# A two-layer encoder trunk on one Trainium2 core: another order of work at the entry of each feed-forward block, and bank sums ahead of weight splits

## What is computed

```python
def rmsnorm(x, g):
    y = x * lax.rsqrt(jnp.mean(x * x, axis=-1, keepdims=True) + EPS)
    return y * g

def conv_gated_ffn(h, w_up, conv_w, conv_b, w_down):
    a = h @ w_up                                   # (1, 512, 1024) @ (1024, 2 * 2816)
    a = depthwise_conv(a, conv_w, width=3, centred) + conv_b
    gate, val = jnp.split(a, 2, axis=-1)
    return (jax.nn.silu(gate) * val) @ w_down

def trunk(x, ...):
    x = x + dilated_attention_mixer(rmsnorm(x, attn_norm_g), ...)          # layer 0
    x = x + conv_gated_ffn(rmsnorm(x, ffn_norm_g[0]), ...)
    x = x + chunk_gmlp_mixer(rmsnorm(x, gmlp_norm_g), ...)                 # layer 1
    x = x + conv_gated_ffn(rmsnorm(x, ffn_norm_g[1]), ...)
    return x
# reference: trunk(x_prompt), trunk(x_sample), each (1, 512, 1024), fp32, shared weights
```

## Time and profile before

| | us |
|---|---|
| median of 3 runs | 2109.98 (2106.78 to 2114.1) |
| profiled execution | 2112.5 |
| its span, first to last instruction | 2110.3 |

### The profile page before, as it was taken

One profiled execution on the slowest core, in us unless ns is written; L12 is line 12 of the kernel. 1 busy time (PEld: TensorE's weight loads), 2 busy tenths in 40 slices (PEclk: granted clock), 3 DMA queues, 4 the chain that ended last, 5 costly groups with the idle time before them and its releaser, 6 DMA issues.

```text
span 2110.3 us, 24700 instructions
## 1 busy us (share of the span) xinstructions
PE 2046.5 (97%) x9316; PEld 1677.6 (79%) x9316; DVE 1248.0 (59%) x1691; ACT 934.3 (44%) x1441; POOL 324.1 (15%) x234
## 2 busy tenths in 40 slices
PE   8999999998999999999999999999899999999999
PEld 8888677886778778787888888888678778778787
DVE  5398774588666666634535344449766666643333
ACT  6233686645444444423434532344544444432221
POOL 0022000341222222000102000223222222100000
PEclk9999899999999999999999999999999999999999
DMA  5111000412432232344343311142252232244444
GB/s 167 31 40 41 16 16 9 142 50 70 160 90 69 81 90 69 126 144 141 135 157 117 80 41 31 51 140 60 60 170 79 71 90 79 73 147 139 133 148 170
DMA packets 181165, 196.48 MB, mean 93 GB/s; under 512 B 8000, under 2 KB 135488, under 8 KB 181056
## 3 DMA queue, kind: packets, MB, share of 16 engines
q1 hardware_dynamic: 180912, 194.80, 29.2%
q10 hardware_dynamic: 144, 0.21, 0.0%
HBM read 159.33 MB, written 35.65 MB: 92 GB/s over the span
## 4 chain that ended last, share of the span: by engine, by line
PE 79%; DVE 12%; issue 4%; ACT 4%; DMA 1%; POOL 0%; SPq 0%; ACTq 0%; DVEq 0%; POOLq 0%
PE bank L766 16%; PE bank L768 16%; PE bank L767 16%; PE bank L539 6%; PE bank L540 6%; PE bank L541 6%; DVE spl L1411 2%; ACT spl L1154 2%; PE bank L690 2%; DVE gate_out L1674 2%; DVE gate_out L1671 2%; PE bank L718 1%; PE bank L701 1%; DVE bank L1655 1%; PE bank L641 1%
## 5 line engine op out<-in xcount | busy, mean ns | idle before, releaser
L766 PE MATMUL bank<-bh,spl 128*128 128x512 f32 x1064 | 421.9, 397 | 41.2 <-DVE bank L1655 23.8
L767 PE MATMUL bank<-bl,spl 128*128 128x512 f32 x1064 | 417.4, 392 | 0.0
L768 PE MATMUL bank<-bh,spl 128*128 128x512 f32 x1064 | 417.3, 392 | 0.0
L766 PEld LDWEIGHTS bank<-bh,spl 128*128 128x128 f32 x1064 | 201.7, 190 | 98.9 <-DVE bank L1655 39.8
L766 PE MATMUL bank<-hid_h,down_h 128*128 128x512 f32 x704 | 275.4, 391 | 4.5 <-DVE x L1796 4.5
L1411 DVE TENSOR_TENSOR hid_l<-hid_w,hid_h 128x1024 fp32r<-128x1024 f32 x88 | 107.8, 1225 | 287.7 <-ACT hid_h L1294 287.7
L767 PE MATMUL bank<-hid_l,down_h 128*128 128x512 f32 x704 | 275.2, 391 | 0.0
L768 PE MATMUL bank<-hid_h,down_l 128*128 128x512 f32 x704 | 274.9, 391 | 0.0
L768 PEld LDWEIGHTS bank<-bh,spl 128*128 128x128 f32 x1064 | 201.6, 189 | 42.6
L767 PEld LDWEIGHTS bank<-bl,spl 128*128 128x128 f32 x1064 | 201.9, 190 | 41.2
L1294 ACT ACTIVATE hid_h<-hid_w 128x1024 fp32r<-128x1024 f32 x88 | 93.2, 1059 | 311.3 <-DMA down_w<-w_down 311.3
(11 more groups left out here) (210 smaller groups left out, 3798.0 us busy)
## 6 DMA issues: line engine op xcount, KB each, us to landing
raw<-w_up SPq DMA_DIRECT2D x88, 512.0 KB, 5.4
hid_w<-hidden_kept SPq DMA_DIRECT2D x88, 512.0 KB, 3.5
hidden_kept<-hidden SPq DMA_DIRECT2D x88, 256.0 KB, 2.3
down_w<-w_down SPq DMA_DIRECT2D x88, 256.0 KB, 3.8
x_kept<-x SPq DMA_DIRECT2D x16, 512.0 KB, 6.5
x<-x_kept SPq DMA_DIRECT2D x16, 512.0 KB, 8.2
gws<-w_in SPq DMA_DIRECT2D x32, 256.0 KB, 3.2
qws<-w_qkv SPq DMA_DIRECT2D x12, 512.0 KB, 3.9
```

The lines of the kernel that those rows point to most:

```text
L766: mm(out, wh, ah, start=first, stop=False, skip_group_check=True)
L767: mm(out, wh, al, start=False, stop=False, skip_group_check=True)
L768: return mm(out, wl, ah, start=False, stop=last, skip_group_check=True)
```

## The change

It reorders; it adds no arithmetic and removes none. Part by part:

1. **Norm statistics.** `norm_cols` comes one half block (12 matmuls) earlier in TensorE's list and `norm_rows` too. VectorE's 4 normalisations of sequence 1 are moved ahead of `scaled(0, 0)` and read bank 4 in place of `rstd`; job 1 therefore waits before its third block for all 12 normalisations, not 8.
2. **Part sums on GpSimd.** T2 and T4 move from VectorE to GpSimd, whose list is now T1, T2, T3, T4 and then the weight sums of job 3. One semaphore (`b_t`) counts all four. P5 is split before P2's blocks, so the counts in `READY` change.
3. **Bank evictions of jobs 0 to 2** and the weight splits between them have another order on ScalarE and VectorE; block 15's split and P4's ScalarE part stand elsewhere in the list.
4. **Windows, jobs 3 to 21.** On VectorE `c22(j)` stands ahead of `w_lo(n0 + 8)`, and `c12(j)` ahead of `w_lo(n0 + 9)` (in job 21 ahead of the tile splits).
5. **First sweep's eviction.** The 8 `evict` stand behind `tile_lo(23)` and no longer behind `tile_lo(24)`.

```diff
--- before.py
+++ after.py
@@ -88,7 +88,7 @@
 NENT = len(ORDER)
 RING = 4
 
-READY = {P1: 4, P2: 8, P5: 9, P6: 10, P3: 11, P7: 12, P4: 13}
+READY = {P1: 4, P5: 5, P2: 9, P6: 10, P3: 11, P7: 12, P4: 13}
 NB = 13
 NADD = 4 * PLAIN + 3 * NWIN
 
@@ -278,8 +278,7 @@
         b_gain = sem("b_gain")
         b_norm = sem("b_norm")
         b_norm12 = sem("b_norm12")
-        b_t13 = sem("b_t13")
-        b_t24 = sem("b_t24")
+        b_t = sem("b_t")
         b_hi = sem("b_hi")
         b_lo = sem("b_lo")
         cp_t1 = sem("cp_t1")
@@ -795,7 +794,7 @@
                         pe.wait_ge(st_root, layer + 1)
                     if j == 1 and q == 2:
                         pe.wait_ge(st_copy, (layer + 1) * NS)
-                        pe.wait_ge(b_norm, layer * 12 + KD)
+                        pe.wait_ge(b_norm, layer * 12 + 12)
                     if j >= 2 and q == 0:
                         pe.wait_ge(hid, (layer * NUP + j - 1) * 2)
                     if j >= 2 and q == 2:
@@ -809,9 +808,9 @@
                             last = triple(bank[:, ((b, c), (a, d))[q // 2][s]], w[:, 0, i], w[:, 1, i],
                                           act[0][:, k, s], act[1][:, k, s], half == 0 and i == 0,
                                           half == 1 and i == HALFK - 1)
-                        if j == 0 and s == 0 and q == 1:
+                        if j == 0 and s == 1 and q == 0:
                             norm_cols(layer, adds)
-                        if j == 0 and s == 0 and q == 2:
+                        if j == 0 and s == 1 and q == 1:
                             norm_rows(layer)
                     last.then_inc(prod, 1)
 
@@ -1222,48 +1221,52 @@
                         A(bh[(P1, P2)[k // HALFK]][:, k % HALFK], x[:, k, 0], ACT.Copy).then_inc(b_hi, 1)
                     hi(6)
                     mid(0, 0)
+                    mid(0, 1)
+                    mid(0, 2)
                     gate(0, 0)
                     hi(7)
-                    mid(0, 1)
-                    mid(0, 2)
+                    mid(0, 3)
+                    act.wait_ge(b_t, layer * 4 + 1)
+                    part(P5, x[:, 0:HALFK, 0])
                     gate(0, 1)
-                    mid(0, 3)
                     hi(8)
+                    mid(1, 0)
                     hi(9)
-                    act.wait_ge(b_t13, layer * 2 + 1)
-                    part(P5, x[:, 0:HALFK, 0])
-                    mid(1, 0)
+                    gate(1, 0)
                     hi(10)
-                    gate(1, 0)
-                    hi(11)
                     mid(1, 1)
                     mid(1, 2)
+                    hi(11)
                     gate(1, 1)
                     mid(1, 3)
                     hi(12)
+                    mid(2, 0)
                     hi(13)
-                    mid(2, 0)
+                    gate(2, 0)
+                    act.wait_ge(prod, w0 + POS[PLAIN - 1, A21] + 1)
+                    act.wait_ge(b_t, layer * 4 + 2)
+                    part(P6, x[:, 0:HALFK, 0])
                     hi(14)
-                    act.wait_ge(prod, w0 + POS[PLAIN - 1, A21] + 1)
-                    act.wait_ge(b_t24, layer * 2 + 1)
-                    part(P6, x[:, 0:HALFK, 0])
                     act.wait_ge(b_norm, layer * 12 + 12)
                     part(P3, x[:, HALFK:KD, 1])
-                    gate(2, 0)
-                    mid(2, 1)
                     act.wait_ge(prod, w0 + POS[PLAIN - 1, A22] + 1)
-                    act.wait_ge(b_t13, layer * 2 + 2)
+                    act.wait_ge(b_t, layer * 4 + 3)
                     part(P7, x[:, 0:HALFK, 1])
-                    mid(2, 2)
-                    act.wait_ge(b_t24, layer * 2 + 2)
-                    part(P4, x[:, HALFK:KD, 0])
 
                 def up_job(j):
 
                     n0, last = POS[j, P1], j == NUP - 1
                     hi(n0 + 3)
-                    mid(j - 1, 3)
-                    copy_t1(j)
+                    if j == PLAIN:
+                        mid(j - 1, 1)
+                        copy_t1(j)
+                        mid(j - 1, 2)
+                        act.wait_ge(b_t, layer * 4 + 4)
+                        part(P4, x[:, HALFK:KD, 0])
+                        mid(j - 1, 3)
+                    else:
+                        mid(j - 1, 3)
+                        copy_t1(j)
                     hi(n0 + 4)
                     gate(j - 1, 1)
                     hi(n0 + 5)
@@ -1702,56 +1705,52 @@
                     for k in range(KD):
                         norm(k, 0, bank[:, 5])
                     dve.wait_ge(st_copy, (layer + 1) * NS)
+                    for k in range(HALFK, KD):
+                        norm(k, 1, bank[:, 4])
                     scaled(0, 0)
                     w_lo(6)
                     for k in range(HALFK):
                         norm_lo(k)
+                    scaled(0, 1)
                     taps(0, 0)
-                    scaled(0, 1)
+                    taps(0, 1)
                     w_lo(7)
-                    for k in range(HALFK, KD):
-                        norm_lo(k)
-                    taps(0, 1)
                     taps(0, 2)
-                    for k in range(HALFK, KD):
-                        norm(k, 1, rstd[:, 1])
+                    part(P5, x[:, 0:HALFK, 0], 9)
                     gated_hidden(0, 1)
                     taps(0, 3)
                     gated_hidden(0, 0)
                     w_lo(8)
                     scaled(1, 0)
+                    for k in range(HALFK, KD):
+                        norm_lo(k)
                     w_lo(9)
-                    part(P5, x[:, 0:HALFK, 0], 9)
                     taps(1, 0)
-                    dve.wait_ge(b_norm, layer * 12 + 12)
-                    V.tensor_tensor(x[:, 0:HALFK, 0], x[:, HALFK:KD, 1], x[:, 0:HALFK, 0], ALU.subtract) \
-                        .then_inc(b_t24, 1)
                     w_lo(10)
-                    dve.wait_ge(b_t24, layer * 2 + 1)
-                    V.tensor_tensor(x[:, HALFK:KD, 0], x[:, HALFK:KD, 0], x[:, 0:HALFK, 0], ALU.subtract) \
-                        .then_inc(b_t24, 1)
                     scaled(1, 1)
+                    taps(1, 1)
                     w_lo(11)
-                    taps(1, 1)
                     taps(1, 2)
                     gated_hidden(1, 1)
                     taps(1, 3)
+                    w_lo(12)
                     gated_hidden(1, 0)
-                    w_lo(12)
                     scaled(2, 0)
                     w_lo(13)
                     taps(2, 0)
+                    part(P6, x[:, 0:HALFK, 0], 10)
                     w_lo(14)
-                    part(P6, x[:, 0:HALFK, 0], 10)
                     part(P3, x[:, HALFK:KD, 1], 11)
                     scaled(2, 1)
+                    w_lo(15)
                     taps(2, 1)
                     part(P7, x[:, 0:HALFK, 1], 12)
 
                 def up_job(j):
 
                     n0, last = POS[j, P1], j == NUP - 1
-                    w_lo(n0 + 3)
+                    if j > PLAIN:
+                        w_lo(n0 + 3)
                     taps(j - 1, 2)
                     w_lo(n0 + 4)
                     taps(j - 1, 3)
@@ -1767,16 +1766,16 @@
                     else:
                         w_lo(n0 + 7)
                     taps(j, 0)
+                    c22(j)
                     if last:
                         tile_lo(1)
                     else:
                         w_lo(n0 + 8)
-                    c22(j)
+                    c12(j)
                     if last:
                         tile_lo(2)
                     else:
                         w_lo(n0 + 9)
-                    c12(j)
                     taps(j, 1)
 
                 def tile_lo(n):
@@ -1809,7 +1808,7 @@
                     gated_hidden(NUP - 1, 0)
                     for n in range(3, NTILE):
                         tile_lo(n)
-                        if n == FT + 2:
+                        if n == FT + 1:
                             for i in range(8):
                                 evict(i)
                         if layer == 0 and FT + 3 <= n < FT + 11:
@@ -1975,9 +1974,14 @@
                                 ALU.mult).then_inc(b_norm12, 1)
                 pool.wait_ge(b_norm12, layer + 1)
                 pool.wait_ge(b_lo, layer * NB + HALFK)
-                G.tensor_tensor(x[:, 0:HALFK, 0], x[:, 0:HALFK, 1], x[:, 0:HALFK, 0], ALU.subtract).then_inc(b_t13, 1)
+                G.tensor_tensor(x[:, 0:HALFK, 0], x[:, 0:HALFK, 1], x[:, 0:HALFK, 0], ALU.subtract).then_inc(b_t, 1)
                 pool.wait_ge(b_norm, layer * 12 + 12)
-                G.tensor_tensor(x[:, 0:HALFK, 1], x[:, HALFK:KD, 1], x[:, 0:HALFK, 1], ALU.subtract).then_inc(b_t13, 1)
+                pool.wait_ge(b_lo, layer * NB + READY[P5])
+                G.tensor_tensor(x[:, 0:HALFK, 0], x[:, HALFK:KD, 1], x[:, 0:HALFK, 0], ALU.subtract).then_inc(b_t, 1)
```

(4 more changed lines are left out.)

## The result

| | before | changed |
|---|---|---|
| median of runs, us | 2112.04 (2106.78 to 2121.43, 4 runs) | 2060.28 (2055.97 to 2063.92, 4 runs) |
| profiled execution, its span | 2112.5, 2110.3 | 2060.13, 2058.3 |
| PE busy, share of the span | 2046.5, 97% | 2029.4, 99% |

The ratio to the kernel before is 0.9749, 95% interval 0.9709 to 0.979. The forecast was 2060, range 2046 to 2080. That the median meets it within 0.3 us is partly luck: medians of the kernel before, taken again with each set of runs, lie between 2106.72 and 2112.04.

What follows compares the result with a forecast made beforehand. PE was taken as the bound, busy 2046.5 of 2110.3 us, its waits ended mostly by c22's eviction. Gains of 25.5 + 10.2 + 8.3 + 6.3 = 50.3 us off 2112.5 gave 2062.2, for a median 2060; range 2046 to 2080.

Steps and rivals of the forecast that it cites:

- windows of jobs 4 to 20: P4 no longer waits for c22 behind a split: 0.75 us in each of 34 windows, 25.5 us.
- job 21: P4 no longer waits for c22 behind a tile split, and the clock stays up: 5.1 us a layer, 10.2 us.
- eviction: First down sweep: tile 22 no longer waits for its bank, nor runs at a lower clock: 4.15 a layer, 8.3 us.
- entry: Start of a feed-forward block to job 3's P4: earlier statistics and new lists bring P4 3.15 us earlier a layer, 6.3 us.
- The tight place: Down tiles want job 21's hidden tile at 879.3, ready about 879.0; up to 1 us a layer may come back.
- the five: Rivals: entry gives nothing 15%, windows give half 12%, order not what P4 awaits 6%, entry gives everything 8%, slower 4%.
- The empty entry: Block entry gives nothing, as POOL sums hold VectorE longer and c11 comes no earlier: 2066 or 2070 us; chance 15%.

Runs made afterwards that it cites:

- entry_only: The changed kernel with the c22/c12 order and the place of the eight evictions undone; ratio to the kernel before 0.9989, both blocks 1403.6 us.
- windows_only: The kernel before with only c22 and c12 moved ahead of the splits in jobs 3 to 21; ratio 0.9808, both blocks 1369.8 us.
- t24_vector: The changed kernel with T2 and T4 moved back from GpSimd to VectorE; both feed-forward blocks 1358.2 us against 1357.6.
- evict_only: The kernel before with only the eight evictions moved behind the split of tile 23; ratio 0.9972, both blocks 1400.4 us.
- starved_splits: The changed kernel with next P2's and P6's splits, and P5's and P7's, moved behind the next job's first taps; both blocks 1403.5 us against 1357.6.

## Why the prediction was right, step by step

| term | forecast, us | measured in the changed kernel | how |
|---|---|---|---|
| windows of jobs 4 to 20 | 25.5 | 25.9 | first P4 to last: 359.53 before, 343.12 after, less the last one's 3.47, in layer 0; twice |
| job 21 | 10.2 | 10.1 | layer 0: P4 late by 0.27 in place of 3.74, 2.85 long in place of 4.44; twice |
| eviction | 8.3 | 8.2 | down stages, 4.18 and 4.04 |
| entry | 6.3 | 7.3 | job 3's P4 after its first matmul: 28.40 before, 24.21 and 25.29 after |
| sum | 50.3 | 51.5 | both blocks: 51.6 |

- **Windows.** The reason was right as written: `c22` was held by the split ahead of it in VectorE's list, not by P7's end, and what comes next (1.4 us of slack) didn't bind.
- **Job 21.** P4's start was right, 0.27 us late against 0.3. The tight place, job 21's hidden tile wanted by the down tiles 0.3 us after it is ready, held: it is ready at 861.5 and wanted at about 861.8.
- **Eviction.** Right in both halves, the idle time and the clock behind it. The second half depends on whether the clock falls: with the evictions at their old place the down stages of the four profiled executions that have them there add up to 7.2 to 8.6 us more than in the changed kernel, by whether it fell in layer 1.
- **Entry.** The list of VectorE, added up, was right to within a microsecond over 60 us: `scaled(2, 1)` starts at 489.98 in a frame that lies 0.35 earlier, so 490.3, where 490.6 was written. The held time was 7.6 us, not 8.3. Both ends of P4's start were seen: in layer 0 the clock did not fall a second time and the gain is 4.2, in layer 1 it did, and the gain is 3.1. The term was taken with the fall in both layers, and is 1.0 too small for that. It also bears the wrong name. It runs to job 3's P4, so it takes in what part 4 does there: in `entry_only`, without part 4, job 3's P4 comes at 26.12 and 26.08 and the gain is 4.6 of the 7.3, and against `windows_only` (27.15 and 26.10) parts 1 to 3 add 3.8. Parts 1 to 3 are worth some 4 us, not 6.3 or 7.3.
- **What was wrong without showing in the sum.** The step credited VectorE with 4.4 us of work taken away and charged it 1.8 us more of held time; `t24_vector` shows that the move is worth 0.6 us over both layers. The sum came out because it was built from the new list as a whole, not from the move.
- **Rivals.** None of the five happened. The empty entry is half true: its reason holds, since what T2 and T4 freed on VectorE was paid back in held splits, and only the earlier statistics kept the entry from being empty.

## What to carry to other kernels

Where TensorE waits at the same place in every round, look at what stands ahead of the awaited instruction in its engine's list and why that one waits: here one swap on an engine with 40% idle time is worth three quarters of the gain. Count a stall of 2 us or more with a fall of the clock behind it, as likely but not certain (last section), and place short evictions ahead of long waits at every change of phase. Before moving work from VectorE to GpSimd, add up both engines' two-input SBUF work in the same stretch; here 2.8 of the 4.4 us that the move freed on VectorE were paid back in held instructions.

## What the runs showed of the hardware that I had not expected

- **The difference between executions sits in a stage that the change doesn't touch.** The first feed-forward block starts at 414.97 before and 414.62 in the changed kernel, but at 422.64 in `evict_only` and 410.53 in `starved_splits`. In the attention stretch of `evict_only` (225 to 340 us) the granted clock is 0.84, in that of `entry_only` 0.94:

```profile
225.00:340.00 115.00, 114.94 (x665) 81.94 (x666) 81.55 (x195) 83.53 (x132) 0.40 (x1) 0.84 0.04 10
```

```profile
225.00:340.00 115.00, 114.33 (x740) 82.03 (x740) 87.78 (x211) 93.18 (x147) 0.24 (x1) 0.94 0.03 9
```

  The same instructions, fewer of them in the same time. Over the 13 profiled executions the block starts between 408.95, at a clock of 0.96, and 422.64, at 0.84. Stage lengths in the blocks differ by up to 2 us between executions where nothing in them was changed (down stage of layer 1, evictions at their old place: 241.71 to 243.54). An effect of 5 us is clear in the stages and lost in the totals.
- **The same idle time may bring the clock down or not.** In the changed kernel P3 of job 3 starts after 2.29 us of idle time in layer 0 and keeps the full clock; in layer 1, after 2.44, the clock goes to 1.2 GHz 1 us after the start and stays there for 3.4 us, eight matmuls 0.43 us apart.

```profile
1464.80 0.50 PE L765 MATMUL bank<-bh,spl 128*128 128x512 f32 x1 [2.44 <-ACT sumsq L1172]
...
1465.83 0.62 PE L766 MATMUL bank<-bl,spl 128*128 128x512 f32 x1
...
1468.81 0.60 PE L767 MATMUL bank<-bh,spl 128*128 128x512 f32 x1
1469.24 0.40 PE L765 MATMUL bank<-bh,spl 128*128 128x512 f32 x1
```

  In the feed-forward blocks of the 13 profiled executions the clock fell behind 13 of 20 idle times of 2.2 to 2.7 us, 6 of 8 of 2.9 us and all 18 of 3.2 us and more; behind the ten of 1.1 to 1.8 us and the 36 of 1.0 us it never did. A fall behind 2.2 to 3.6 us made the next 24 matmuls take 1.5 to 1.8 us longer where no other wait followed.
- **VectorE and GpSimd take turns.** T3 and T4, issued while a VectorE split waited or ran, took 5.07 and 4.95 us, not 4.62, and the waiting split ran between T2 and T3: two GpSimd sums in a row let one VectorE instruction through in between.
